# Block 1's first pair of a two-block transformer kernel: one low part by a negated cast and an accumulating DMA, two sums read from PSUM, another order in the lead-in

## The chip, the cores and the metric

One core of a Trainium2 chip runs the whole program in one launch. The metric is the device time of that core in microseconds (us). A profiled execution gives each engine's instructions with their times, counted from the first instruction of the span.

## The reference, cut to what matters

Two transformer blocks run one after the other on 256 tokens of width 1024, in float32. The change lies in block 1, whose two layers each have two SwiGLU feed-forwards around a mixer, so four feed-forwards in all:

```python
def _swiglu(x, w1, w3, w2):
    return (jax.nn.silu(x @ w1) * (x @ w3)) @ w2

for l in range(DEPTH):                                    # DEPTH = 2
    h = _swiglu(x, ffn_w1[l, 0], ffn_w3[l, 0], ffn_w2[l, 0])   # "which" 0
    x = _layernorm(ALPHA * x + 0.5 * h, ...)
    h = _mixer(x, l, ...)
    x = _layernorm(ALPHA * x + h, ...)
    h = _swiglu(x, ffn_w1[l, 1], ffn_w3[l, 1], ffn_w2[l, 1])   # "which" 1
    x = _layernorm(ALPHA * x + 0.5 * h, ...)
```

x is 256 x 1024, w1 and w3 are 1024 x 2816, w2 is 2816 x 1024.

## The kernel before, in words

**Every product is three.** A float32 operand is split in a high part (ScalarE casts it to fp32r) and a low part (VectorE subtracts the high part from the original and writes fp32r). TensorE then multiplies high by high, high by low and low by high. So every 1 MB unit of weights (128 partitions x 2048 values) costs one cast of ScalarE and one subtraction of VectorE before TensorE may use it. Weights go through a ring of four slots: `w_raw` (loaded by SyncE's queue), `w_high`, `w_low`. The semaphores `slot_full`, `slot_hi` and `slot_lo` count the three steps for each slot. SyncE's next load into a slot waits until the low part of the unit before is made.

**How a feed-forward is cut.** The 2816 hidden columns are 11 blocks of 256. Blocks 0, 1, 4, 7 and 10 are computed plainly: units `h0_0`, `h0_1` and so on hold w1 and w3 of a block and half of the rows (`_0` rows 0 to 511, `_1` rows 512 to 1023), and `d0` holds its rows of w2. The other six blocks are three groups of two, called quads. In a quad, the hidden products for both 128-token tiles and both halves of the rows are made by seven products and not eight, as in Strassen's and Winograd's method. Their weight units are b11, b21, v, x, w, y and b22. They come from four raw pieces that SyncE's queue loads beside the ring: R11 and R21 (of w1; tiles `buf_v` and `buf_q`), R12 and R22 (of w3; `buf_u` and `buf_val`). VectorE's `add_to` makes, in place in R11, the sums R11+R12 (for v), then +R22 (for x), then +R21 (for y). GpSimd makes R12+R22 (for w) with an accumulating DMA from `buf_val` into `buf_u` (line 712) once the first of these sums is done. So R11 as loaded must have been read for b11 before the first `add_to` may overwrite it.

**The forms.** The other operands of v, x, w and b22 are four combinations of the activations, the forms. VectorE's `whole` (line 2707) rebuilds x's transpose as high plus low in a quarter of `mix_param`, `combine` (2711) forms a difference or sum of two quarters, ScalarE casts it into `form_high` (1981) and VectorE makes `form_low` (2715).

**The lead-in.** This is the stretch of each feed-forward before and in its first quad: block 0 (hidden of token tile 0, then tile 1), block 1, the transposes of block 0's activations, d0, transposes of block 1, then b11, b21, v, x, d1 for tile 0, w, d1 for tile 1, y, b22. Each engine works through an order written out by hand:

- TensorE as just said. Block 1's tile 0 needs the low part of h1_0 and `multiply(0,0)`; its tile 1 needs `multiply(0,1)`; x and w need their own low parts, w also ScalarE's copy `term2` (line 2011).
- ScalarE: the casts of x's transpose for tile 1, Silu of block 0 tile 0 (`activate(0,0)`, line 1952), casts of h1_0 and h1_1 (1844), Silu of tile 1, casts of d0 and b11 (1942), four forms, then it waits for R21 and casts b21, then Silu of block 1 tile 0, the cast of the transposes (1957), Silu of tile 1, casts of v, x and the rest.
- VectorE: low parts of x's transpose (2510), two `whole`, `multiply(0,0)` (2682), low of h1_0 (2504), two `whole`, two `combine`, `multiply(0,1)`, low of h1_1, two `combine`, low of d0, form 0, `multiply(1,0)`, low of the transposes (2688), forms 1 to 3, low of b11 (2673), `multiply(1,1)`, `add_to` R12 (2678), low of b21, low of v, low of the transposes, `add_to` R22, low of x, low of d1, `add_to` R21, low of w, y and b22.
- GpSimd: for each feed-forward two loads of `ln_param`, then for each quad a wait for the first sum and for R22, and the DMA of line 712.

The transposes of x for token tile 1 lie in the PSUM banks `aux[:, 2, :]` and `aux[:, 3, :]` (rows 0 to 511 and 512 to 1023).

Of the kernel before, what the change touches and what calls it, by code (L numbers as in the profile page):

```python
# [10 lines left out]
ALU = mybir.AluOpType  # L11
ACT = mybir.ActivationFunctionType
# [74 lines left out]
FFN_UNIT, FFN_USES, FFN_LOADS, FFN_DONE = ffn_units()  # L87
# [154 lines left out]
def build(nc, a, out, stop=None):  # L242
    ctx = ExitStack()
    with ctx:
        def sb(name, shape, dt=F32):
            return ctx.enter_context(nc.sbuf_tensor(name, shape, dt))

        def sem(name):
            return ctx.enter_context(nc.semaphore(name))
# [4 lines left out]
        wlo = sb("w_low", [P, RING, UNIT], F32R)  # L254
# [16 lines left out]
        ident = sb("ident", [P, P])  # L271
# [12 lines left out]
        nz = sb("newton_t", [P, 48])  # L284
# [16 lines left out]
        def flat(t):  # L301
            return t[:, :, :].rearrange("p t d -> p (t d)")
# [7 lines left out]
        quarter = [flat(mix_par)[:, k * NC:(k + 1) * NC] for k in range(4)]  # L310
        term1, term2, term3, silu1 = quarter
        FORM_AT = (1, 0, 2, 3)
        R11, R21, R12, R22 = range(4)
        sum_raw = [flat(t) for t in (bv, bq, bu, bval)]
# [11 lines left out]
        aux = ctx.enter_context(nc.psum_tensor("aux", [P, 4, NC], F32))  # L326
# [4 lines left out]
        slot_lo = [sem(f"slot_lo{s}") for s in range(RING)]  # L331
# [3 lines left out]
        aux_read = [sem(f"aux_read{b}") for b in range(4)]  # L335
# [9 lines left out]
        r_full = [sem(f"r_full{r}") for r in range(4)]  # L345
        sum_done = sem("sum_done")
        w_sum = sem("w_sum")
        form_done = sem("form_done")
        form_hi = sem("form_hi")
        form_lo = sem("form_lo")  # L350
# [19 lines left out]
        ident_in = sem("ident_in")  # L370
# [101 lines left out]
        def ffn_n(l, which, s):  # L472
            return l * SLOT_LAYER[s] + (FFN_USES[s] + CH // 2) * which
# [8 lines left out]
        def ffn_unit(l, which, name):  # L482

            s, n = FFN_UNIT[name][0:2]
            return s, ffn_n(l, which, s) + n
# [5 lines left out]
        def quads_before(l, which, q):  # L491
            return QUADS * (2 * l + which) + q
# [170 lines left out]
        def _(pool):  # L663
# [41 lines left out]

            def sums_by_dma(l, which):

                for q in range(QUADS):
                    n = quads_before(l, which, q)
                    pool.wait_ge(sum_done, 3 * n + 1)  # L710
                    pool.wait_ge(r_full[R22], 16 * n + 16)
                    pool.dma_start(sum_raw[R12], sum_raw[R22], accum_op=ALU.add).then_inc(w_sum, 16)
# [41 lines left out]
            n = 0  # L754
# [1081 lines left out]
        def _(act):  # L1836
# [92 lines left out]
            def ffn1(l, which, tile1, next_tile0, mid):  # L1929

                aux0 = [c.k for c in n_aux]

                def used(name):
                    act.wait_ge(unit_used, ffn_done(l, which, name))

                def high_plain(name):
                    s, _, n, _ = FFN_UNIT[name]
                    high(s, ffn_load(l, which, s) + n)

                def high_sum(name, q, r):  # L1940
                    s = FFN_UNIT[f"{name}_{q}"][0]
                    nc.scalar.copy(whi[:, s, :], sum_raw[r]).then_inc(slot_hi[s], 1)  # L1942
# [7 lines left out]
                def activate(i, t):  # L1950
                    act.wait_ge(aux_full[t], aux0[t] + PLAIN.index(i) + 1)
                    nc.scalar.activation(act_b[:, t, 0:FB], aux[:, t, 0:FB], ACT.Silu).then_inc(act_done, 1)

                def plain_high_T(i):
                    act.wait_ge(aux_full[2], aux0[2] + FFN_T[i] + 1)
                    _, src, (k, tok) = place_pair(2, 0)
                    nc.scalar.copy(yTh[:, k, tok], src).then_inc(t_hi, 1)
# [7 lines left out]
                def last_high(t):  # L1965
                    act.wait_ge(aux_full[2 + t], aux0[2 + t] + FFN_AUX[2 + t])
                    nc.scalar.copy(yTh[:, 2:4, t * P:(t + 1) * P],
                                   aux[:, 2 + t, 0:2 * P].rearrange("p (f c) -> p f c", f=2)).then_inc(t_hi, 1)

                tile1()  # L1970
                aux0[2:] = [n_aux[2].k, n_aux[3].k]
                activate(0, 0)
                high_plain("h1_0")
                high_plain("h1_1")
                activate(0, 1)
                high_plain("d0")
                loaded(0, R11)
                high_sum("b11", 0, R11)
                for n in range(FORMS):
                    act.wait_ge(form_done, FORMS * (2 * l + which) + n + 1)  # L1980
                    nc.scalar.copy(form_h[:, n, :, :].rearrange("p k c -> p (k c)"), quarter[FORM_AT[n]])\
                        .then_inc(form_hi, 1)
                used("h1_0")
                loaded(0, R21)
                high_sum("b21", 0, R21)
                activate(1, 0)
                plain_high_T(0)
                activate(1, 1)
                summed(0, 1)
                high_sum("v", 0, R11)  # L1990
# [209 lines left out]
            l = L2  # L2200
# [295 lines left out]
        def _(dve):  # L2496
# [3 lines left out]
            V = nc.vector  # L2500
# [161 lines left out]
            def ffn1(l, which, tile1, k_norm, next_tile0, mid, half_first):  # L2662

                aux0 = []
                act0 = NT * len(PLAIN) * (2 * l + which)

                def low_plain(name):
                    low(*ffn_unit(l, which, name))

                def low_sum(name, q, r):  # L2670
                    s, n = ffn_unit(l, which, f"{name}_{q}")
                    dve.wait_ge(slot_hi[s], n + 1)
                    V.tensor_tensor(wlo[:, s, :], sum_raw[r], cast(whi[:, s, :]), ALU.subtract)\  # L2673
                        .then_inc(slot_lo[s], 1)

                def add_to(q, r, other):
                    dve.wait_ge(r_full[other], 16 * quads_before(l, which, q) + 16)
                    V.tensor_tensor(sum_raw[r], sum_raw[r], sum_raw[other], ALU.add).then_inc(sum_done, 1)  # L2678

                def multiply(i, t):  # L2680
                    dve.wait_ge(act_done, act0 + NT * PLAIN.index(i) + t + 1)
                    V.tensor_tensor(gate_b[:, t, 0:FB], act_b[:, t, 0:FB], aux[:, t, FB:2 * FB], ALU.mult)\
                        .then_inc(aux_read[t], 1)
# [20 lines left out]
                def whole(t, half, at):  # L2704

                    k, tok = slice(4 * half, 4 * half + 4), slice(t * P, (t + 1) * P)
                    V.tensor_tensor(quarter[at].rearrange("p (k c) -> p k c", k=4), cast(xTh[:, k, tok]),
                                    cast(xTl[:, k, tok]), ALU.add)

                def combine(at, one, two, op):  # L2710
                    V.tensor_tensor(quarter[at], quarter[one], quarter[two], op).then_inc(form_done, 1)  # L2711
# [7 lines left out]
                tile1()  # L2719
                dve.drain()  # L2720
                h0 = n_hi.k
                whole(1, 0, 0)
                whole(1, 1, 1)
                multiply(0, 0)
                low_plain("h1_0")
                whole(0, 0, 2)
                whole(0, 1, 3)
                dve.drain()
                combine(1, 0, 1, ALU.subtract)
                dve.drain()  # L2730
                combine(0, 2, 0, ALU.subtract)
                multiply(0, 1)
                low_plain("h1_1")
                combine(2, 1, 2, ALU.subtract)
# [6 lines left out]
                plain_low_T(0)  # L2741
                for n in range(1, FORMS):
                    form_low(n)
                low_sum("b11", 0, R11)
                multiply(1, 1)
                add_to(0, R11, R12)
                low_sum("b21", 0, R21)
                for q in range(QUADS):
# [326 lines left out]
            l = L2  # L3075
# [502 lines left out]
```

## Time and profile before

| what | value |
| --- | --- |
| median of 3 runs | 1946.69 us (1946.23 to 1947.9) |
| the profiled execution, its own time | 1946.73 us |
| its span, first to last instruction | 1944.7 us |
| TensorE busy | 1896.4 us, 98% of the span |
| VectorE busy | 1405.9 us, 72% |
| ScalarE busy | 1000.5 us, 51% |
| mean granted TensorE clock | 0.996 of full |
| lead-ins, about | 15 to 75, 455 to 512, 642 to 700, 1082 to 1140 us |

The time outside the span is 1946.73 - 1944.7 = 2.0 us. A line such as `466.87 1.90 ACT L1844 CAST w_high<-w_raw ...` in a timeline gives the start, the length, the engine (PE TensorE, DVE VectorE, ACT ScalarE, POOL GpSimd), the line of the kernel, and what is written and read; brackets give the idle time of the engine before it and what ended it. Neighbouring instructions of an engine overlap by about 0.1 us, so that a row "x2" of 3.70 us is two casts that start 1.80 us apart.

### The profile page before, as it was taken

Reading aid. Unit: us, or ns where it says so; the run is one execution under the profiler, and the core shown is the slowest. Engines: PE = TensorE matmul, PEld = TensorE weight load, DVE = VectorE, ACT = ScalarE, POOL = GpSimd, SP = SyncE. Lnnn points to the kernel's source line nnn. Section 1 sums busy time; section 2 is a strip of 40 time slices with the busy share of each in tenths; the row PEclk is TensorE's granted clock in tenths of the full one; section 3 lists DMA queues with packets and bytes.
Section 4 is the critical chain, followed back from the end, with each engine's and each line's share of the span. In section 5 each row is a group of like instructions: output and inputs, shape, how many; then the busy total and the mean of one; then the engine's idle time right before and its main releaser. Section 6 shows DMA issues by size and latency. Waiting matters only on the chain.

```text
span 1944.7 us, 23187 instructions
## 1 busy us (share of the span) xinstructions
PE 1896.4 (98%) x9016; PEld 1553.2 (80%) x9016; DVE 1405.9 (72%) x1599; ACT 1000.5 (51%) x1203; POOL 108.4 (6%) x176
## 2 busy tenths in 40 slices
PE   8999999999999999999999999989999999999999
PEld 6788788887788778878888778877788887778887
DVE  6887766778887888777667988878755466775545
ACT  4555444544555455543554455557544355654443
POOL 2001100000000000110000000011000000100000
PEclk9999999999999999999999999999999999999999
DMA  9764554447764666565345766365465555346542
GB/s 345 230 217 167 199 191 173 148 156 260 230 222 145 226 216 216 187 215 196 131 173 165 246 216 217 125 170 174 136 227 173 172 179 178 120 152 211 182 163 87
DMA packets 177729, 366.39 MB, mean 188 GB/s; under 512 B 7408, under 2 KB 51360, under 8 KB 176096
## 3 DMA queue, kind: packets, MB, share of 16 engines
q1 hardware_dynamic: 170512, 334.85, 49.9%
q0 software_dynamic: 7120, 30.21, 6.0%
q8 instruction: 66, 1.08, 0.2%
q14 instruction: 31, 0.25, 0.0%
HBM read 351.39 MB, written 1.05 MB: 181 GB/s over the span
## 4 chain that ended last, share of the span: by engine, by line
PE 82%; DVE 11%; ACT 3%; DVEq 2%; DMA 1%; issue 1%; SPq 0%; ACTq 0%
PE acc L834 49%; PE aux L834 16%; PE aux L1110 10%; DVE w_low L2504 3%; DVE w_low L2673 2%; DVE buf_v L2678 1%; PE aux L849 1%; DMA buf_q<-ffn_w 1%; ACT w_high L1942 1%; PE aux L945 1%; PE aux L1242 1%; DVEq L2556 1%; DVE xT_low L2510 1%; PE aux L1073 1%; DVE mix_param L2711 0%
## 5 line engine op out<-in xcount | busy, mean ns | idle before, releaser
L2504 DVE TENSOR_TENSOR w_low<-w_raw,w_high 128x2048 fp32r<-128x2048 f32 (+2 forms) x268 | 604.2, 2267 | 208.5 <-ACT w_high L1844 205.0
L1844 ACT CAST w_high<-w_raw 128x2048 fp32r<-128x2048 f32 (+2 forms) x268 | 502.9, 1893 | 249.4 <-PE acc L834 207.7
L834 PE MATMUL acc<-w_high,yT_high 128*128 128x512 f32 (+1 forms) x836 | 331.6, 397 | 3.0 <-DVE yT_low L2688 2.5
L834 PE MATMUL acc<-w_high,yT_low 128*128 128x512 f32 (+1 forms) x836 | 326.0, 390 | 0.0
L834 PE MATMUL acc<-w_low,yT_high 128*128 128x512 f32 (+1 forms) x836 | 325.6, 389 | 0.0
L834 PE MATMUL acc<-w_high,xT_high 128*128 128x512 f32 (+2 forms) x752 | 298.0, 396 | 7.0 <-DVE xT_low L2510 4.5
L834 PE MATMUL acc<-w_high,xT_low 128*128 128x512 f32 (+2 forms) x752 | 291.4, 388 | 0.0
L834 PE MATMUL acc<-w_low,xT_high 128*128 128x512 f32 (+2 forms) x752 | 291.1, 387 | 0.0
L834 PE MATMUL aux<-w_high,xT_high 128*128 128x512 f32 x576 | 229.9, 399 | 7.2 <-DVE w_low L2504 4.5
L834 PE MATMUL aux<-w_high,xT_low 128*128 128x512 f32 x576 | 225.3, 391 | 0.0
L834 PE MATMUL aux<-w_low,xT_high 128*128 128x512 f32 x576 | 224.7, 390 | 0.0
L834 PEld LDWEIGHTS acc<-w_high,yT_high 128*128 128x128 f32 x836 | 157.6, 188 | 38.5 <-issue 6.5
L834 PEld LDWEIGHTS acc<-w_high,yT_low 128*128 128x128 f32 x836 | 157.3, 188 | 32.9
L834 PEld LDWEIGHTS acc<-w_low,yT_high 128*128 128x128 f32 x836 | 157.8, 189 | 30.6
L834 PEld LDWEIGHTS acc<-w_high,xT_high 128*128 128x128 f32 x752 | 141.7, 188 | 41.0 <-DVE xT_low L2510 5.2
L1942 ACT CAST w_high<-buf_v 128x2048 fp32r<-128x2048 f32 x48 | 91.8, 1913 | 153.4 <-DVE buf_v L2678 110.4
L834 PEld LDWEIGHTS acc<-w_high,xT_low 128*128 128x128 f32 x752 | 141.6, 188 | 28.8
L834 PEld LDWEIGHTS acc<-w_low,xT_high 128*128 128x128 f32 x752 | 141.8, 189 | 26.2
L2673 DVE TENSOR_TENSOR w_low<-buf_v,w_high 128x2048 fp32r<-128x2048 f32 x48 | 109.9, 2289 | 55.6 <-ACT w_high L1942 55.6
L834 PEld LDWEIGHTS aux<-w_high,xT_high 128*128 128x128 f32 x576 | 108.5, 188 | 32.9 <-issue 8.5
L834 PEld LDWEIGHTS aux<-w_high,xT_low 128*128 128x128 f32 x576 | 108.4, 188 | 23.2
L834 PEld LDWEIGHTS aux<-w_low,xT_high 128*128 128x128 f32 x576 | 108.6, 189 | 20.9
(385 smaller groups left out, 2329.1 us busy)
## 6 DMA issues: line engine op xcount, KB each, us to landing
w_raw<-w_ff SPq DMA_DIRECT2D x64, 1024.0 KB
w_raw<-w_in SPq DMA_DIRECT2D x52, 1024.0 KB
w_raw<-ffn_w SPq DMA_DIRECT2D x44, 1024.0 KB
w_raw<-ffn_w SPq DMA_DIRECT2D x78, 512.0 KB
w_raw<-w_branch SPq DMA_DIRECT2D x16, 1024.0 KB
buf_v<-ffn_w SPq DMA_DIRECT2D x12, 1024.0 KB, 9.1
buf_u<-ffn_w SPq DMA_DIRECT2D x12, 1024.0 KB, 6.0
buf_q<-ffn_w SPq DMA_DIRECT2D x12, 1024.0 KB, 6.9
```

Of the source, the lines that this page charges most:

```text
L834: last = nc.tensor.matmul(dst, lhs[:, kt, tok], rhs(j), start=(kt == k_first and q == 0), stop=(kt == k_last and q == 2))
L849: last = nc.tensor.transpose(aux[:, b, k * P:(k + 1) * P], src[:, t, kt * P:(kt + 1) * P], ident[:])
L945: last = nc.tensor.transpose(aux[:, b, (2 * f + t) * P:(2 * f + t + 1) * P], gate_b[:, t, f0:f0 + P], ident[:])
L1073: last = nc.tensor.transpose(aux[:, b, (2 * f + t) * P:(2 * f + t + 1) * P], h[:, f0:f0 + P], ident[:])
L1110: last = nc.tensor.matmul(aux[:, b, :], lhs(k), rhs[:, s, k * NC:(k + 1) * NC], start=(first and k == 0 and n == 0), stop=(k == 3 and n == ...
L1242: last = nc.tensor.transpose(aux[0:width, b, (2 * k + t) * P:(2 * k + t + 1) * P], src(t, h), ident[:])
L1844: nc.scalar.copy(whi[:, s, 0:size], raw[:, s, 0:size]).then_inc(slot_hi[s], 1)
L1942: nc.scalar.copy(whi[:, s, :], sum_raw[r]).then_inc(slot_hi[s], 1)
L2504: V.tensor_tensor(wlo[:, s, 0:size], raw[:, s, 0:size], cast(whi[:, s, 0:size]), ALU.subtract)\
L2510: V.tensor_tensor(dst_l[:, k, tok], src, cast(dst_h[:, k, tok]), ALU.subtract)\
L2556: dve.drain()
L2673: V.tensor_tensor(wlo[:, s, :], sum_raw[r], cast(whi[:, s, :]), ALU.subtract)\
```

## The change

- GpSimd and ScalarE make the low part of `b11_0`, the b11 of a feed-forward's first quad: ScalarE writes -R11, cast to fp32r, into the `w_low` slot, then a DMA that GpSimd issues adds R11 onto it. GpSimd waits until that DMA has landed and then raises `slot_lo`. VectorE's `low_sum("b11", 0, R11)` is gone, and VectorE waits for that `slot_lo` before `add_to(0, R11, R12)`.
- Of the four `whole` of VectorE the two for tile 1 are gone. ScalarE copies `aux[:, 3, :]` into a quarter, and two subtractions of VectorE read `aux[:, 2, :]` directly.
- ScalarE runs a Silu on one column of `ident` ahead of the lead-in, and casts h1_0 before `activate(0,0)`. VectorE takes h1_0's low part before `multiply(0,0)`.
- ScalarE does `activate(1,0)` and the cast of the transposes before it waits for R21 and casts b21. Its wait for `h1_0` used is gone.
- VectorE does `multiply(1,1)` right after the forms.

```diff
@@ GpSimd, sums_by_dma
+                n = 2 * l + which
+                s = FFN_UNIT["b11_0"][0]
+                pool.wait_ge(b11_neg, n + 1)
+                pool.dma_start(wlo[:, s, :], sum_raw[R11], accum_op=ALU.add).then_inc(b11_sum, 16)
+                pool.wait_ge(b11_sum, 16 * n + 16)
+                pool.sem_inc(slot_lo[s], 1)
@@ ScalarE, ffn1
+                act.wait_ge(ident_in, 16)
+                nc.scalar.activation(nz[:, 0:1], ident[:, 0:1], ACT.Silu)
                 tile1()
                 aux0[2:] = [n_aux[2].k, n_aux[3].k]
+                high_plain("h1_0")
                 activate(0, 0)
-                high_plain("h1_0")
+                act.wait_ge(aux_read[3], aux0[3] + 1)
+                nc.scalar.copy(quarter[1], aux[:, 3, :]).then_inc(form_in, 1)
                 high_plain("h1_1")
                 activate(0, 1)
                 high_plain("d0")
                 loaded(0, R11)
                 high_sum("b11", 0, R11)
+                nc.scalar.activation(wlo[:, FFN_UNIT["b11_0"][0], :], sum_raw[R11], ACT.Copy, scale=-1.0)\
+                    .then_inc(b11_neg, 1)
                 for n in range(FORMS):
...
-                used("h1_0")
+                activate(1, 0)
+                plain_high_T(0)
                 loaded(0, R21)
                 high_sum("b21", 0, R21)
-                activate(1, 0)
-                plain_high_T(0)
                 activate(1, 1)
@@ VectorE, ffn1
-                whole(1, 0, 0)
-                whole(1, 1, 1)
+                low_plain("h1_0")
                 multiply(0, 0)
-                low_plain("h1_0")
                 whole(0, 0, 2)
                 whole(0, 1, 3)
+                dve.wait_ge(form_in, 2 * l + which + 1)
+                V.tensor_tensor(quarter[1], aux[:, 2, :], quarter[1], ALU.subtract).then_inc(form_done, 1)
                 dve.drain()
-                combine(1, 0, 1, ALU.subtract)
-                dve.drain()
-                combine(0, 2, 0, ALU.subtract)
+                V.tensor_tensor(quarter[0], quarter[2], aux[:, 2, :], ALU.subtract).then_inc(form_done, 1)
                 multiply(0, 1)
...
                     form_low(n)
-                low_sum("b11", 0, R11)
                 multiply(1, 1)
+                s, n = ffn_unit(l, which, "b11_0")
+                dve.wait_ge(slot_lo[s], n + 2)
                 add_to(0, R11, R12)
                 low_sum("b21", 0, R21)
```

## Rows read from the trace of the kernel before

**Rows 1.** Whole page, busy time and share of the span of TensorE.

```profile
PE 1896.4 (98%) x9016; PEld 1553.2 (80%) x9016; DVE 1405.9 (72%) x1599; ACT 1000.5 (51%) x1203; POOL 108.4 (6%) x176
```

**Rows 2.** Waits of TensorE: total, times, longest (us), whole span.

```profile
PE aux L1110 <- DVE w_low L2673: 10.0, 4, 2.8
...
PE aux L834 <- DVE w_low L2504: 4.5, 5, 1.1
...
PE acc L834 <- DVE yT_low L2688: 2.5, 1, 2.5
...
PE aux L1110 <- ACT mix_param L2011: 2.2, 2, 1.1
```

**Rows 3.** Timeline of VectorE, second lead-in: start, length, engine, line.

```profile
461.44 0.69 DVE L2510 TENSOR_TENSOR xT_low<-aux,xT_high 128x512 fp32r<-128x512 f32 x1 [1.06 <-ACT xT_high L1849]
...
464.93 2.29 DVE L2504 TENSOR_TENSOR w_low<-w_raw,w_high 128x2048 fp32r<-128x2048 f32 x1 [1.08 <-ACT w_high L1844]
467.14 1.29 DVE L2707 TENSOR_TENSOR mix_param<-xT_high,xT_low 128x512 f32<-128x512 f32 x2
...
479.61 2.28 DVE L2673 TENSOR_TENSOR w_low<-buf_v,w_high 128x2048 fp32r<-128x2048 f32 x1
...
482.14 2.29 DVE L2678 TENSOR_TENSOR buf_v<-buf_v,buf_u 128x2048 f32<-128x2048 f32 x1
...
493.61 2.29 DVE L2673 TENSOR_TENSOR w_low<-buf_v,w_high 128x2048 fp32r<-128x2048 f32 x1 [1.98 <-ACT w_high L1942]
```

**Rows 4.** Timeline of ScalarE, second lead-in.

```profile
461.42 1.28 ACT L1952 ACT_TABLE_LOAD   x1
...
463.00 3.70 ACT L1844 CAST w_high<-w_raw 128x2048 fp32r<-128x2048 f32 x2
466.60 0.38 ACT L1952 ACTIVATE buf_k<-aux 128x256 f32<-128x256 f32 x1
466.87 1.90 ACT L1844 CAST w_high<-w_raw 128x2048 fp32r<-128x2048 f32 x1
```

**Rows 5.** Timeline of TensorE, second lead-in.

```profile
467.37 0.47 PE L834 MATMUL aux<-w_high,xT_high 128*128 128x512 f32 x1 [1.11 <-DVE w_low L2504]
```

**Rows 6.** Stages: PE, PEld, DVE, ACT, POOL busy, clock, DMA share, GB/s.

```profile
474.00:477.00 3.00, 3.00 (x17) 2.51 (x16) 2.95 (x3) 3.00 (x4) 0.00 (x0) 1.00 0.84 341
486.00:491.00 5.00, 5.00 (x24) 4.13 (x23) 5.00 (x4) 0.85 (x2) 0.00 (x0) 1.00 1.03 210
498.00:500.00 2.00, 2.00 (x7) 1.51 (x6) 2.00 (x2) 0.00 (x0) 0.00 (x0) 0.50 0.26 29
```

**Rows 7.** Line L712, the accumulating DMA, all twelve.

```profile
DMA to landing us min/median/max: 6.9/7.0/8.7
```

**Rows 8.** Timeline of GpSimd, second lead-in.

```profile
484.73 0.90 POOL L712 DMA_DIRECT2D buf_u<-buf_val  x1 [24.34 <-DVE buf_v L2678]
```

**Rows 9.** DMA issues of 459 to 461 us.

```profile
ln_param<-ln_g POOLq DMA_DIRECT2D x1, 512.0 KB, 6.8
ln_param<-ln_b POOLq DMA_DIRECT2D x1, 512.0 KB, 8.7
```

**Rows 10.** DMA issues, whole span.

```profile
ln_param<-mix_norm POOLq DMA_DIRECT2D x1, 512.0 KB, 4.1
```

**Rows 11.** Timeline of ScalarE, first lead-in.

```profile
28.24 1.92 ACT L1942 CAST w_high<-buf_v 128x2048 fp32r<-128x2048 f32 x1
...
35.35 1.90 ACT L1942 CAST w_high<-buf_q 128x2048 fp32r<-128x2048 f32 x1 [3.12 <-DMA buf_q<-ffn_w]
```

**Rows 12.** Timeline of VectorE, first lead-in.

```profile
42.98 2.29 DVE L2678 TENSOR_TENSOR buf_v<-buf_v,buf_u 128x2048 f32<-128x2048 f32 x1
```

**Rows 13.** Timeline of ScalarE, third lead-in.

```profile
655.77 1.91 ACT L1844 CAST w_high<-w_raw 128x2048 fp32r<-128x2048 f32 x1
```

**Rows 14.** Timeline of VectorE, third lead-in.

```profile
669.76 2.29 DVE L2678 TENSOR_TENSOR buf_v<-buf_v,buf_u 128x2048 f32<-128x2048 f32 x1
```

**Rows 15.** Timeline of VectorE, fourth lead-in.

```profile
1108.76 2.28 DVE L2678 TENSOR_TENSOR buf_v<-buf_v,buf_u 128x2048 f32<-128x2048 f32 x1
```

More of the change, by code:

```diff
@@ L347, in build @@
         w_sum = sem("w_sum")
+        b11_neg = sem("b11_neg")
+        form_in = sem("form_in")
+        b11_sum = sem("b11_sum")
         form_done = sem("form_done")
```

## The prediction

> **What bounds the kernel now.** I read the page first: TensorE is busy for 98% of the span [rows 1], so only its waits, under 50 us, can be had. The list of TensorE's waits then says where they are [rows 2]. Four of them, 10.0 us in all, one in each feed-forward, are before product x of the first quad (line 1110, waiting for the low part of line 2673). Twice the copy of line 2011 holds w for 1.1 us. Block 1 waits for the low part of h1_0 for 1.1 us in three lead-ins (the second one's is [rows 5]), and once d0 waits for 2.5 us (first lead-in). Together this is about 18 us, the most that the change can touch: 0.9%.
>
> The timelines of VectorE and ScalarE of the second lead-in [rows 3, 4] say what is behind the wait before x. VectorE adds R12 to R11 from 482.14; from there to the end of x's low part at 493.61 + 2.29 = 495.90 it is a fixed chain of 13.8 us: add, low of b21, low of v, low of the transposes, add, ScalarE's cast of x, low of x. The product w hangs on the same chain one `add_to` and one cast later. The change alters nothing in this chain. So **a lead-in becomes shorter by what its first `add_to` (line 2678) comes earlier**, and by nothing else, as long as TensorE still waits for x. Call its start A: it is 42.98, 482.14, 669.76 and 1108.76 in the four lead-ins [rows 3, 12, 14, 15]. The second and fourth are one pattern, 626.6 us apart.
>
> **The parts that make TensorE's early waits go.** ScalarE's table load of 1.28 us, now between the cast of x's transpose and the Silu [rows 4], moves into idle time ahead of the lead-in; if it couldn't be hidden there it would cost what it costs now. With h1_0's cast ahead of the Silu too, that cast starts at about 461.4 and not 463.00, and the low part ends at 465.6, before TensorE ends block 0 at 467.37 - 1.11 = 466.26 [rows 5]. The wait of 1.1 us goes, in three lead-ins. The third has no such wait and gains nothing here. VectorE's two `whole` (0.60 us each by the pair of [rows 3]) become one ScalarE copy that fits between two casts; reading PSUM in a subtraction costs VectorE no more than SBUF: its low part of x's transpose reads PSUM and takes 0.69 us [rows 3], and I take the same for the new subtractions (bounds 0.6 and 0.7, no matter for the sum). All this puts TensorE up to 1.4 us ahead in block 1. But what goes here comes back before x, unless A moves as well.
>
> The Trainium skill (ScalarE: Activation LUTs, What ACT_TABLE_LOAD costs) gives a switch of tables 2.66 us, load and drain. Here the Silu begins right behind the 1.28 us, so the trace has no such drain; by the page's figure the early wait would shrink by 1.4 us more, and the sum would be the same.
>
> **The part that moves A.** VectorE loses the low part of b11, 2.20 us of its time (line 2673 at 479.61, [rows 3]). In its place A waits for this chain, second lead-in: TensorE ends block 0 at 466.3; Silu of tile 1 to 466.6, as before [rows 4]; then casts at a spacing of 1.80 us (the pair of 3.70 us in [rows 4]): d0 from 466.6, b11 from 468.4, the negated cast from 470.2 to 472.1. The trace has no negated cast; a plain one of this size takes 1.90, and I take that. (Bounds: 1.9, and 2.3 if it were as slow as VectorE's.) Then 0.3 us until GpSimd begins the DMA, as now from the end of the add at 484.43 to 484.73 [rows 3, 8]; T for the DMA to land; and 0.3 us, my estimate from the same step, for GpSimd to raise the semaphore. So A = 472.7 + T. Without this DMA VectorE would be free by 480: its forms end at 479.61 already before, and everything ahead of them is earlier. So T decides as soon as it is over 7.3 us.
>
> **T.** The same kind of DMA, same size, same engine, landed 6.9 to 8.7 us after its issue, median 7.0 [rows 7]. Those run in stretches where nothing is loaded: in 486 to 491 us the DMA engines are full (1.03) with it alone, at 210 GB/s [rows 6]. It is 5 us of all the engines' time, twice what a load of 1 MB costs (341 GB/s at a share of 0.84 in 474 to 477). The new one starts at 472.4 in the second lead-in, where the loads of d2 and d3 want most of the engines. Below, T is 7.0. Above, with even sharing against loads all the time, it is 7.0 + 5 = 12. Between them: if turns go by bytes, the loads get a third, 2.5 us more, so 9.5; if the turns favour the transfer with the larger pieces, less. Two `ln_param` loads on the same queue, put into a full DMA at 459, landed after 6.8 and 8.7 us [rows 9], one in a quieter place after 4.1 [rows 10]: they don't stand in line behind SyncE's loads, they push in. I take T = 8.4, both ends kept for the range.
>
> **The sum.** Second lead-in: A = 481.1 for 482.14, **1.0 us won**. Fourth, the same pattern: **1.0 won**. Third: ScalarE's cast of d0 is at 655.77 [rows 13] and doesn't come earlier, as TensorE doesn't there; the negated cast ends at 655.77 + 3.60 + 1.91 = 661.3, A = 661.9 + 8.4 = 670.3 for 669.76, **0.5 lost**. First: b11's cast starts at 28.24 [rows 11], held by d0's arrival, which doesn't change, so the negated cast ends at 31.95 and T = 8.4 would give A = 41.0, 2.0 earlier. But R21 is on its way then: it landed at 35.3, ScalarE waited 3.12 us for it [rows 11]. With 5 us of DMA work pushed in ahead of it it lands at 40.3; the cast of b21 is over at 42.2, `activate(1,1)` is queued behind it on ScalarE, `multiply(1,1)` behind that, and VectorE gets to A at 42.9 to 43.0, for 42.98: **nothing won**. (If R21 isn't held up: 2.0 more.) There the new order does make d0 start about 3 us earlier, for `activate(1,0)` no longer stands behind R21, and TensorE stands before the transposes and x instead.
>
> Total: 1.0 + 1.0 - 0.5 + 0 = 1.5 us. In general the second to fourth lead-ins give 26.8 - 3T: 5.8 us at T = 7.0, nothing at 8.9. TensorE's own wait for b11's low part is met in time: from 466.3 it has 72 products at about 0.22 us (24 in 5 us, [rows 6]) and eight short transposes to do first, so it gets there at about 483.4. Queued behind VectorE's new wait are the low parts of b21 and v, which TensorE needs 4.4 and 6.6 us after A: 485.6 and 487.8, before it gets there at 486.2 and 488.9, twelve products apart. The next DMA of GpSimd (line 712) needs the first sum anyway, so it isn't held up. R22 and the loads behind it have many us to spare in the last three lead-ins.
>
> TensorE's clock: after the wait before x it fell to 0.50, the lower of its two levels (1.2 and not 2.4 GHz), in 498 to 500 us [rows 6]. In the new kernel the wait before x is about 0.4 us longer in the second and fourth, so the low clock can come in more lead-ins. As w then waits less for its copy (1.1 us where the clock stayed, [rows 2]), this costs some tenths of a us each; I leave it out of the sum and in the range.
>
> From the profiled execution's 1946.73 (span 1944.7 and 2.0 around it; the median of the runs is 1946.69, the same within 0.04): 1946.73 - 1.5 = **1945.2 us**.
>
> **Rivals.** (1) *The DMA is as quick as its median, T = 7.0.* For it speaks that the loads leave gaps at 0.84; against it, that none of the twelve rows behind that median shares the engines with loads. It gives 5.8 us, 1940.9; with R21 not held up A is 39.6 in the first lead-in, 3.4 more, 1937.5. Down to T = 7.6 or with R21 on time the kernel is faster by over 0.2% (3.9 us). Chance 0.3. (2) *The DMA shares evenly and becomes the bound,* T = 11: A is 483.7, 672.9 and 1110.3, and 43.6 in the first, so 1.6 + 3.1 + 1.6 + 0.6 = 6.9 us lost, 1953.6. It is one mechanism: VectorE, which has the low parts of b21 and v queued behind, stands for a transfer. It is slower than before from T = 8.9 and by over 0.2% from 10.2. Chance 0.15, as no row shows this DMA beside loads. The Trainium skill (DMA: Bandwidth & Descriptors, Queues, rings and completion order) says that each DMA engine goes round between the queues it has work for, a packet at a time. By that rule, even turns in time would give this rival's 1953.6; that the software queue isn't held behind SyncE's agrees with [rows 9]. (3) *It does nothing:* the gains of the early part are given back before x and A moves by less than a us each way; this is my forecast's case, with chance 0.55.
>
> **Numbers.** 0.2% of 1946.7 is 3.9 us, about what a measurement of this kernel can tell from no change. Faster 0.3, within 0.55, slower 0.15. The likeliest case's own range is 1942.8 to 1948. The range to hold 8 in 10 takes in most of rival 1 and the start of rival 2: 1938.5 to 1950.8.
>
> **What would show it.** Right: no wait of TensorE for h1_0's low part; VectorE idle for 2 to 3 us before line 2678 in the last three lead-ins, released by GpSimd; the new DMA landing in 8 to 9 us; x waiting 2.5 to 3.5 us. In the first lead-in ScalarE waits for R21 until about 40. Wrong: a landing near 7 or over 10, R21 on time, or a wait before x that vanishes, which would mean that the chain from A isn't fixed.

## The result: slower, outside the predicted range

The changed kernel takes 1952.03 us (median of 13 runs, 1949.54 to 1955.25), the kernel before 1947.50 beside it (13 runs, 1946.23 to 1948.48): a ratio of 1.0024, 95% interval 1.0016 to 1.0033. That is 4.5 us slower. I had forecast 1945.2 in 1938.5 to 1950.8, and gave "slower" a chance of 0.15. The profiled execution took 1950.31 us, 3.6 more than that of before; over the 13 runs TensorE's mean granted clock goes from 0.990 to 0.996, and the profiled one (0.996) is among the quickest.

The page after, TensorE against [rows 1]; TensorE's work is the same, its waits are not:

```profile
span 1948.5 us, 23191 instructions
...
PE 1896.9 (97%) x9016; PEld 1553.3 (80%) x9016; DVE 1392.4 (71%) x1587; ACT 1010.2 (52%) x1215; POOL 113.6 (6%) x180
```

TensorE's waits after, to be laid beside [rows 2] (in total, times, longest; lines 843 and 1119 were 834 and 1110 before):

```profile
PE aux L1119 <- DVE w_low L2687: 18.4, 8, 3.6
...
PE acc L843 <- DVE w_low L2518: 3.4, 4, 2.0
...
PE aux L1119 <- POOLq L716: 2.0, 2, 1.6
PE aux L843 <- DVE w_low L2518: 1.2, 2, 0.6
```

The early part of the change did what it should: the wait for h1_0's low part (now line 2518) fell from 4.5 to 1.2 us in the group of [rows 2], and the copy that held w (2.2 us) is gone from the list. All of it came back, and more, at the products of the first quad: 10.0 us became 18.4. Of these, 14.2 us are the four waits before x (3.5 to 3.6 us each, for 2.0 to 2.8 before) and 4.2 us are four new ones before b21. On top, b11 waits for the new DMA itself in the first and the third lead-in (1.6 and 0.4 us, the row with POOLq). The waits of VectorE name the new holder, four times, once in each feed-forward:

```profile
DVE buf_v L2692 <- POOLq L716: 17.9, 4, 5.3
```

Line 2692 is the `add_to` whose start I called A (2678 before), and line 716 is where GpSimd raises `slot_lo`, once the new DMA has landed. The DMA's own line:

```profile
L714 POOL DMA_DIRECT2D w_low<-buf_v x4: 878/898/917, 32.1 to 1101.8; - x4
...
DMA to landing us min/median/max: 9.6/10.6/11.5
```

That is T: 9.6 to 11.5 us, median 10.6, for the 8.4 of my sum. The timeline of VectorE gives A itself, for [rows 12, 3, 14, 15] (in brackets the idle time before, and what ended it):

```profile
43.28 2.29 DVE L2692 TENSOR_TENSOR buf_v<-buf_v,buf_u 128x2048 f32<-128x2048 f32 x1 [5.30 <-POOLq L716]
...
482.13 2.29 DVE L2692 TENSOR_TENSOR buf_v<-buf_v,buf_u 128x2048 f32<-128x2048 f32 x1 [3.41 <-POOLq L716]
...
672.77 2.29 DVE L2692 TENSOR_TENSOR buf_v<-buf_v,buf_u 128x2048 f32<-128x2048 f32 x1 [5.28 <-POOLq L716]
...
1112.00 2.29 DVE L2692 TENSOR_TENSOR buf_v<-buf_v,buf_u 128x2048 f32<-128x2048 f32 x1 [3.94 <-POOLq L716]
```

The lead-ins themselves begin 0.06, 1.25 and 2.79 us later than before from the second on, by the start of TensorE's transposes. In each lead-in's own time A has moved by +0.30, -0.07, +1.76 and +0.45 us: 2.4 of the 3.8 us by which the span grew. The rest is at product x and behind it: x's twelve products take 1.57, 0.90 and 1.59 us longer in the first, second and fourth lead-in (0.07 less in the third), against which w's two waits of 1.1 us are gone. Here is x in TensorE's timeline of the second lead-in and in the stages with its clock (columns as in [rows 6]):

```profile
496.04 0.76 PE L1119 MATMUL aux<-w_high,form_high 128*128 128x512 f32 x1 [3.54 <-DVE w_low L2687]
```

```profile
496.00:498.00 2.00, 1.96 (x5) 1.60 (x6) 2.00 (x1) 1.65 (x1) 0.00 (x0) 0.50 0.04 8
498.00:500.00 2.00, 2.00 (x6) 1.53 (x5) 2.00 (x2) 0.00 (x0) 0.00 (x0) 0.50 0.24 48
500.00:502.00 2.00, 2.00 (x6) 1.59 (x5) 2.00 (x2) 1.59 (x1) 0.00 (x0) 0.51 1.02 343
```

After an idle 3.54 us the clock is at its lower level (0.50) for all of x in this lead-in. x's twelve products took 5.46 us (496.04 to 501.50), for 4.56 before, where the same wait was 2.66 us and the first four products still ran at full clock. This lead-in lost 1.19 us although A had not moved at all.

What the steps ahead of T did, in the timeline of ScalarE (compare [rows 4]):

```profile
453.32 1.28 ACT L1980 ACT_TABLE_LOAD   x1 [2.25 <-PE acc L843]
...
461.36 1.92 ACT L1853 CAST w_high<-w_raw 128x2048 fp32r<-128x2048 f32 x1
...
468.43 1.91 ACT L1951 CAST w_high<-buf_v 128x2048 fp32r<-128x2048 f32 x1
470.24 1.91 ACT L1992 ACTIVATE w_low<-buf_v 128x2048 fp32r<-128x2048 f32 x1
```

The table load is hidden, h1_0's cast starts at 461.36 (forecast 461.4), the negated cast takes 1.91 us and ends at 472.15 (forecast 472.1). GpSimd issues at 472.45, 0.3 us later, as assumed. Up to there every step is in its place; the transfer is not.

### The profile page after: what moved, and what is told of

It is laid out like the page before. It is cut to its first block, busy times and chain, and to the rows that moved or that the text cites. A ratio compares the mean times of both kernels' runs of the same rounds, so it can differ in the third digit from the quotient of the medians.

```text
span 1948.5 us, 23191 instructions
## 1 busy us (share of the span) xinstructions
PE 1896.9 (97%) x9016; PEld 1553.3 (80%) x9016; DVE 1392.4 (71%) x1587; ACT 1010.2 (52%) x1215; POOL 113.6 (6%) x180
## 4 chain that ended last, share of the span: by engine, by line
PE 80%; DVE 8%; issue 5%; DMA 3%; ACT 3%; DVEq 1%; POOL 0%; SPq 0%; POOLq 0%
PE acc L843 48%; PE aux L843 16%; PE aux L1119 9%; DMA w_low<-buf_v 2%; DVE w_low L2518 2%; DVE w_low L2687 1%; DVE buf_v L2692 1%; PE aux L858 1%; DMA w_raw<-ffn_w 1%; ACT w_high L1951 1%; PE aux L954 1%; PE aux L1251 1%; DVEq L2570 1%; DVE xT_low L2524 1%; PE aux L1082 0%
## 5 line engine op out<-in xcount | busy, mean ns | idle before, releaser
L2687 DVE TENSOR_TENSOR w_low<-buf_v,w_high 128x2048 fp32r<-128x2048 f32 x44 | 100.8, 2290 | 55.9 <-ACT w_high L1951 55.9
```

## The experiments

Each kernel ran beside the kernel before on one chip; "A" is given for the first to the fourth lead-in. In one table:

```
kernel             median us  ratio, 95% interval       landing, us       A, us
after              1952.03    1.0024 [1.0016, 1.0033]   11.1 9.6 11.5 10.1   43.28 482.13 672.77 1112.00
e1 no DMA          1938.11    0.9954 [0.9940, 0.9967]   -                    37.91 475.21 662.69 1100.01
e2 DMA alone       1957.23    1.0052 [1.0038, 1.0066]   11.1 to 12.0         42.77 484.75 675.43 1116.62
e3 loads held      1939.16    0.9962 [0.9948, 0.9975]   10.4 7.0 7.0 7.0     42.49 478.73 663.44 1099.55
e4 order alone     1939.19    0.9963 [0.9949, 0.9977]   -                    38.14 476.20 662.57 1100.40
e6 R21 order alone 1943.91    0.9983 [0.9974, 0.9992]   -                    39.34 478.72 665.03 1103.92
e7 h1_0 alone      1944.10    0.9986 [0.9977, 0.9995]   -                    43.89 481.78 668.25 1105.78
e8 half the DMA    1940.77    0.9968 [0.9955, 0.9981]   8.4 to 9.4           40.31 477.62 665.64 1102.31
e9 loads held late 1941.07    0.9973 [0.9962, 0.9983]   11.2 7.0 8.9 6.9     43.58 479.71 666.32 1102.50
e5 mixed           1934.32    0.9933 [0.9920, 0.9947]   - 7.0 7.0 6.9        37.75 473.96 660.19 1096.32
```

The kernel before had 1946.91 beside e1 to e4, 1947.26 beside e5 to e8 and 1946.72 beside e9. Landings and A are those of the one profiled execution of each kernel. The theory is that the DMA, late beside the loads, sets A and takes more than the rest gains; the rival, that the new order in the lead-in is what costs.

**e1: everything but the DMA.** VectorE makes the low part again, ahead of `multiply(1, 1)`.

```diff
-                nc.scalar.activation(wlo[:, FFN_UNIT["b11_0"][0], :], sum_raw[R11], ACT.Copy, scale=-1.0)...
...
+                low_sum("b11", 0, R11)
                 multiply(1, 1)
...
-                dve.wait_ge(slot_lo[s], n + 2)
```

> The changed kernel without the negated cast and the accumulating DMA: VectorE makes b11's low part itself again, all other edits stay. Theory (the DMA alone costs, through the start A of the first add_to): VectorE is free when its forms are done, adds 2.2 us for the low part, and A comes 3.4 us earlier than in the kernel before in the first lead-in and 1.2 to 1.4 us in each of the other three, so about 7 us less than before: 1940 us, if TensorE's low clock does not appear more often. Rival (the new orders or the reads of PSUM cost): the time stays at 1950 to 1952 us.

It gave 1938.11, 8.8 us faster than the kernel before beside it. As the whole change is 4.5 us slower, its DMA costs 13.3 us. A comes 5.1, 6.9, 7.1 and 8.8 us earlier than before; most of it is won in the first lead-in and carried on. In each lead-in's own time it is 4.7, 1.6, 1.5 and 1.6 us, more than the 3.4 and 1.2 to 1.4 expected. Waits of TensorE:

```profile
PE aux L1113 <- DVE w_low L2679: 11.1, 4, 3.2
```

So x still waits, 2.65 us in the last three. The wait was moved there and not removed, but from an A that is earlier.

**e2: the DMA alone**, put into the kernel before: the negated cast after `high_sum("b11", 0, R11)`, GpSimd's five lines, and VectorE's wait in the place of `low_sum("b11", 0, R11)`.

> The kernel before with nothing but the negated cast and the accumulating DMA in place of VectorE's low part of b11. Theory (the DMA alone costs): it is issued within 0.3 us of where the changed kernel issues it in the second and third lead-in, lands 9.6 to 11.5 us later, and the time is that of the changed kernel, 1950 to 1952 us. Rival (the new orders cost): VectorE is relieved of 2.2 us and the time is 1946 to 1948 us, no more than before.

It gave 1957.23, 10.3 us slower than before and 5 more than the theory's upper figure. The direction is settled, the size was a miss: here all four landings are over 11 us (11.1, 12.0, 11.5, 11.8), not only the first and third. In the second and fourth lead-in SyncE issues a load of 1 MB 0.16 us ahead of the DMA here, 1.38 us ahead of it in the changed kernel; the table under e9 shows what that does.

```profile
DMA to landing us min/median/max: 11.1/11.6/12.0
```

**e3: the DMA with the loads behind it held back.** SyncE waits for the sum before the loads that stand behind R22.

```diff
                     quad_load(l, which, 0, r)
+                sp.wait_ge(b11_sum, 16 * (2 * l + which) + 16)
                 for q in range(QUADS):
```

> The changed kernel, where the sync engine waits for the new DMA before it issues the first load behind R22, so that in the last three lead-ins no weight load is under way beside it. Theory (loads beside it stretch it): it lands 7.0 us after issue in the last three lead-ins, A comes 2.5 to 4.5 us earlier there than in the changed kernel, and with about the same first lead-in the time is 1942 to 1944 us. Rival (this DMA is slow by itself, for its fp32r destination or its place): it still takes 9.6 us or more and the time stays at 1950 us or above.

It gave 1939.16, better than expected. The DMA's line and VectorE's A (second lead-in):

```profile
DMA to landing us min/median/max: 7.0/7.0/10.4
```

```profile
478.73 2.29 DVE L2693 TENSOR_TENSOR buf_v<-buf_v,buf_u 128x2048 f32<-128x2048 f32 x1 [0.74 <-POOLq L717]
```

One wait on the queue of loads, and the same DMA lands in 7.0 us in the last three lead-ins. In the first it can't help: what is under way there stands ahead of the wait, and the landing is 10.4 us. VectorE's idle time ahead of A is 0.74 us, where it was 3.4 to 5.3. And x waits 1.4 to 1.5 us in these three, with its products at full clock (0.47 us for the first one, for 0.76 above):

```profile
492.64 0.47 PE L1120 MATMUL aux<-w_high,form_high 128*128 128x512 f32 x1 [1.46 <-DVE w_low L2688]
```

In each lead-in's own time A comes 0.7, 2.7, 4.5 and 3.2 us earlier than in the changed kernel, 11.0 of the 12.3 us by which the span is shorter; the rest would be x's products.

The wait on the queue is not free. The held loads are now issued just ahead of GpSimd's next DMA, the one that makes w's sum (now line 722), and in the second lead-in that lands after 12.7 us, for the 7.0 of [rows 7]:

```profile
DMA to landing us min/median/max: 12.7/12.7/12.7
```

ScalarE waited 1.7 us for it, and no wait of TensorE names it. And e3 is not faster than e1, which has no such DMA (1938.11): what the quiet DMA gains over VectorE's low part in the last three lead-ins it loses in the first.

**e4: the order alone.** e1 with the four `whole` copies and the SBUF subtractions of the kernel before in the place of the sums from PSUM.

> As e1, and the two sums are made from the rebuilt transposes again as before (four wholes, no copy by ScalarE, no read of PSUM): only the orders and the early table load are left of the change. Theory: the two wholes for tile 1 lie in the time in which VectorE waits for the cast of h1_0, so this kernel is within 1 us of e1. Rival: the sums from PSUM save VectorE 1.2 us in each lead-in, so this kernel is 4 to 5 us slower than e1.

It gave 1939.19, so reading PSUM directly is worth 1.1 us, and the new order 7.7. The 1.1 is small: the intervals of the two ratios overlap, though all five runs of e1 (up to 1938.53) lie below all five of e4 (from 1938.83).

**e6 and e7: the order in two halves**, each put into the kernel before. e6 has `activate(1, 0)` and `plain_high_T(0)` ahead of the wait for R21; e7 has the table load and h1_0's cast ahead of the Silu, and `low_plain("h1_0")` ahead of `multiply(0, 0)`.

```diff
-                used("h1_0")
-                loaded(0, R21)
-                high_sum("b21", 0, R21)
                 activate(1, 0)
                 plain_high_T(0)
+                loaded(0, R21)
+                high_sum("b21", 0, R21)
```

> The kernel before with one edit: ScalarE does the Silu and the cast of the transposes of block 1's tile 0 before it waits for R21. Theory: only the first lead-in gains, as only there R21 is late; VectorE's idle 3.8 us before that tile's product goes and A comes 3.5 to 5 us earlier: 1942 to 1943.5 us. Rival (the gain of e4 is from the early cast of h1_0): no change, 1946 to 1947 us.

> The kernel before with only the early table load and h1_0's cast and low part ahead of the first Silu and product. Theory: nothing in the first lead-in (R21 sets A there) and up to 1.3 us earlier A in the second and fourth, about 0 in the third: 1944 to 1945.5 us. Rival (the waits that go come back before x): no change, 1946 to 1947 us.

They gave 1943.91 (0.4 over the expected range) and 1944.10, 3.3 and 3.2 us won; e4, which has both, has 7.7, 1.2 more than the two added up. e6's gain is in the first lead-in, whose A is at 39.34 for 42.98, and stays at 3.4 to 4.8 in the later ones. In e7 the first A is even 0.9 later, but in this profile the first weights came late and TensorE's first transposes of the lead-in began 1.7 us later too, so in the lead-in's own time A is 0.8 earlier; the others gain 1.2, 1.0 and 1.2 (about 0 was expected in the third). I had written that what goes in block 1 comes back before x unless A moves, and then counted as if A stayed. It doesn't: VectorE's last work ahead of A is `multiply(1, 1)`, which waits for block 1's products, so A moved with them.

**e8: half the bytes.** The DMA makes 512 KB of the low part, VectorE the other half.

```diff
-                pool.dma_start(wlo[:, s, :], sum_raw[R11], accum_op=ALU.add).then_inc(b11_sum, 16)
+                pool.dma_start(wlo[:, s, 0:D], sum_raw[R11][:, 0:D], accum_op=ALU.add).then_inc(b11_sum, 16)
...
+                pool.wait_ge(b11_half, n + 1)
```

> The changed kernel where ScalarE negates and the DMA adds only half of b11's low part (512 KB) and VectorE makes the other half (1.1 us). If the late start of the DMA's data is a fixed price beside loads (3 to 4 us from issue to first data, as in the changed kernel's trace, and then by size), it lands after 6.5 to 7.5 us; if all of it stretches with the size, after 5 to 5.5 us. In both cases A comes 3 to 5 us earlier than in the changed kernel in each lead-in, and the time is 1938 to 1941 us.

The time came out as expected (1940.77), the landing not: 8.4 to 9.4 us for half the bytes, where the whole takes 7.0 with no loads beside it. Nor did A: in each lead-in's own time it comes 3.2, 1.5, 1.3 and 2.5 us earlier than in the changed kernel, where 3 to 5 was expected. So its own bytes are not the main part of what makes the landing long: halving them takes off 0.7 to 2.4 us. The trace's packet records show where the time is. From GpSimd's issue to the DMA's first data packet, from there to its last one, and what SyncE's loads moved in between:

```
kernel, issue at       first packet   data     loads meanwhile
after        32.10     +4.28          6.33     0.57 MB
after       472.45     +2.86          6.28     0.50
after       661.24     +4.35          6.48     0.63
after      1101.80     +2.74          6.89     0.69
e3          471.70     +1.47          5.19     0
e3          656.39     +1.45          5.17     0
e8 (half)   468.60     +4.40          4.02     0.63
e8 (half)   656.12     +4.41          4.58     0.83
```

With the engines to itself the DMA's first packet comes 1.5 us after its issue and its data take 5.2 us. Beside the loads it starts 1.3 to 2.9 us later, and the whole DMA then runs 1.1 to 1.7 us longer. The stages around it say the same (second lead-in, the last two columns are DMA share and GB/s):

```profile
473.00:474.00 1.00, 1.00 (x6) 0.83 (x5) 1.00 (x1) 1.00 (x3) 0.36 (x1) 1.00 0.97 395
474.00:475.00 1.00, 1.00 (x8) 0.85 (x7) 1.00 (x2) 0.54 (x2) 0.00 (x0) 1.00 1.04 422
...
476.00:477.00 1.00, 1.00 (x7) 0.79 (x5) 1.00 (x3) 1.00 (x1) 0.00 (x0) 1.00 1.11 233
477.00:478.00 1.00, 1.00 (x6) 0.84 (x5) 1.00 (x3) 0.63 (x2) 0.00 (x0) 1.00 1.02 213
...
481.00:482.00 1.00, 1.00 (x7) 0.81 (x6) 0.00 (x0) 0.00 (x0) 0.00 (x0) 1.00 0.96 393
```

At 395 to 422 GB/s the loads run alone, though the DMA was issued at 472.45; at 213 to 233, with the engines just as full, it is the new DMA's turn. Compare e3, where 474 to 476 is this DMA alone:

```profile
474.00:476.00 2.00, 2.00 (x12) 1.68 (x10) 1.85 (x4) 1.95 (x3) 0.00 (x0) 1.00 0.97 197
```

**e9: the wait of e3, two loads later**, so that the loads of d2 and d3 may still be under way.

```diff
                     hidden1(l, which, o, 0)
+                    if q == 0:
+                        sp.wait_ge(b11_sum, 16 * (2 * l + which) + 16)
                     for name in late_downs(q):
```

> As e3, but the sync engine's wait stands two loads later: d1 and h4_0 (2 MB) may go out beside the new DMA, only d2 and d3 are held back. In the second and fourth lead-in h4_0 is through at about the issue of the new DMA, in the third it runs 2 to 3 us longer. If only loads that run beside it stretch the new DMA, it lands after 7.0 to 7.5 us in the second and fourth and after 8.5 to 9.5 us in the third, and the time is 1939.5 to 1942 us, with e3's 1939.2 below. If d2 and d3 were not what held it up (rival: any backlog of the loads' queue does, or the DMA's own price), it lands after 9 us or more in all, and the time is 1947 us or more.

All of it came as expected: 7.0 and 6.9 us in the second and fourth lead-in, 8.9 in the third, 1941.07 us. By the packet records nothing of the loads was left beside the transfer in the second and fourth, and 0.10 MB in the third. The place in the program is the same as in the changed kernel; the loads under way are what differs.

The same records show what the start hangs on. In the second and fourth lead-in the last load that SyncE issued ahead of the DMA stands at another distance in each kernel, and the first packet follows it:

```
kernel   last load issued ahead of the DMA by   first packet of the DMA after its issue
e9       6.43 us                                1.47  1.46 us
after    1.38                                   2.86  2.74
e8       0.52                                   4.40  4.37
e2       0.16                                   5.04  5.09
```

In the changed kernel's second lead-in the 256 packets of 4 KB of that load (1 MB, issued at 471.07) run from 472.1 to 476.0, and the DMA's first one comes at 475.3. The load issued 2.2 us *after* the DMA stands back in turn: no load has a packet under way from 476.2 to 478.9. In the third lead-in more of the loads is still to be moved, and the first packet comes at 4.3 to 4.4 us in the changed kernel, e2 and e8.

**e5: what the runs point to.** The first feed-forward makes the low part on VectorE (as e1), the other three by the DMA with the loads held back (as e3).

```diff
+                if (l, which) == (0, 0):
+                    low_sum("b11", 0, R11)
                 multiply(1, 1)
+                if (l, which) != (0, 0):
+                    s, n = ffn_unit(l, which, "b11_0")
+                    dve.wait_ge(slot_lo[s], n + 2)
```

> The first feed-forward as in e1 (VectorE makes b11's low part, no negated cast, no DMA), the other three as in e3 (DMA, with the loads behind R22 waiting for it). Theory (each lead-in's share follows its A alone): A comes at 37.9 in the first lead-in as in e1, 4.6 us earlier than in e3, the rest stays as in e3: 1934 to 1935.5 us, below every kernel so far. Rival (the first lead-in's gain is given back later, or e1 and e3 gain the same microseconds): 1938 us or more.

It gave 1934.32, ratio 0.9933 [0.9920, 0.9947]: 12.9 us faster than before where the change as it was made is 4.5 slower, and the best kernel of this study. Its page, TensorE's waits and VectorE's A (second lead-in):

```profile
PE 1892.9 (98%) x9016; PEld 1552.2 (80%) x9016; DVE 1394.1 (72%) x1588; ACT 1009.1 (52%) x1214; POOL 112.7 (6%) x179
```

```profile
PE aux L1122 <- DVE w_low L2691: 7.6, 4, 3.0
...
PE aux L1122 <- ACT mix_param L2029: 3.3, 3, 1.1
```

```profile
473.96 2.29 DVE L2696 TENSOR_TENSOR buf_v<-buf_v,buf_u 128x2048 f32<-128x2048 f32 x1 [0.80 <-POOLq L719]
```

TensorE's wait before x is 7.6 us in all, for 14.2 in the changed kernel, 11.1 in e1 and 10.0 before. w waits 1.1 us for its copy three times, where it was twice before and not at all in the changed kernel.

## Why the prediction was wrong

**The step that failed is T, the landing time of the new DMA, 8.4 in the sum.** It was 9.6 to 11.5. I had taken it between its quiet 7.0 and an even sharing of the engines with the loads, which adds 5 us, and went below the middle, since two smaller loads in [rows 9] "push in". Both ends priced only how the engines are shared, once both transfers move. That this part has the right size is luck: the data took 1.1 to 1.7 us longer, and 8.4 had 1.4 for it. What I had no term for is that the first packet comes 1.3 to 2.9 us later while loads are under way. The rows had a hint of it: 512 KB took 6.8 us in a full DMA [rows 9] and 4.1 in a quieter place [rows 10], 2.7 us more for half the bytes. I read them for the order in which transfers run and not for the delay. With the four measured landings in the place of 8.4 the recorded sum loses 0.7, 0.2, 3.6 and 0.6 us and gives 1951.8, against 1950.31 in the profiled run: T alone turns the forecast from faster to slower.

**Which rival it was.** The second: the DMA becomes what VectorE waits for, with T near 11. A follows at once: issue plus landing is 472.45 + 9.6 = 482.05 for A at 482.13, and the other three agree to 0.1 us (the 0.3 us that I added for GpSimd's semaphore isn't there). The rival's 1953.6 was for T = 11 in all four; the landings were 11.1, 9.6, 11.5 and 10.1, and the profiled run has 1950.31. Its mechanism, even sharing of the engines' time, was not what happened: in the time of the DMA's 128 packets of 8 KB ran 136 to 184 of the loads', mostly 4 KB at 0.16 to 0.17 us each. Where both transfers move, they go about one for one: from 478.8 to 480.3 us start 31 packets of the DMA and 31 of the loads. With one such turn for each of the DMA's packets, 16 engines would need 128 / 16 x 0.17 = 1.4 us more, an estimate that falls in the 1.1 to 1.7 measured. It isn't shown to be the cause of all of it: the data took 6.50 us in e9's third lead-in with 0.10 MB of loads beside them, and two of the twelve transfers behind [rows 7] took 6.65 and 6.81 us with none, each with its last one to three packets well after the rest.

The Trainium skill (DMA: Bandwidth & Descriptors, Queues, rings and completion order) describes turns between the queues, a packet at a time, and those one-for-one stretches agree with it; I had priced them as equal time, 5 us. The start does not come out of turns: in the 1.3 to 2.9 us by which it is late the DMA gets none, while the loads' packets run.

**The first lead-in.** I wrote that R21 would be pushed back to 40.3 and set A at 43.0. R21 landed at 35.3, as before; ScalarE waited 0.73 us for it:

```profile
35.34 1.91 ACT L1951 CAST w_high<-buf_q 128x2048 fp32r<-128x2048 f32 x1 [0.73 <-DMA buf_q<-ffn_w]
```

The new DMA's first packet came at 36.4, once R21 was in. R21 went first, and the DMA waited for its turn. A came out at 43.28 for my 43.0, a right number by luck, for a wrong reason: T was 11.1 and set it alone.

**The third lead-in.** I had written that ScalarE's cast of d0 (655.77) "doesn't come earlier". It began at 655.42, though the lead-in itself began 1.25 us later (0.85 by its second group of transposes), so in its own time it was 1.2 to 1.6 us early. The DMA was issued at 661.24 and not 661.6, and T = 11.5 took that back and more. e7, which has the early cast of h1_0 alone, also brings A 1.0 us forward in this lead-in, where I had nothing.

**Behind A.** I had b11, b21 and v in time for TensorE. With T = 11.1 and 11.5 b11 is late itself (1.6 and 0.4 us), and b21 is late in all four lead-ins, by 0.3 to 1.5 us.

**VectorE's idle time.** In the first lead-in VectorE stood free from 37.98, the end of its last work ahead of A, and idle for 5.3 us; in e1, with the low part of b11 to make as well, it begins A at 37.91.

**The clock.** I left it out as some tenths of a us in each lead-in. The second one lost 1.19 us with A unmoved, 0.9 of it in x's products, and x's products of the first and fourth, at full clock before, lost 1.6 us each, most of which the missing wait of w gave back. Over the span 1.4 of the 3.8 us are not in A. The runs' mean clock, 0.990 to 0.996, goes with their times (1955.25 us at 0.990, 1949.98 at 0.996), and the median lies 1.7 us above the profiled run. That more lead-ins have low stretches in the other runs would explain it, but only the profiled one has a trace.

**The early part** I had put at nothing, on the ground that only A counts. That A counts is right in the main, but VectorE's work ahead of A follows block 1's products, so an earlier block 1 moves A: e7 gains 3.2 us by it. And R21's order alone, which brings A from 42.98 to 39.34 in the first lead-in (e6), gains 3.3. So there were 8.8 us to win and 13.3 to lose where the sum had 1.5 to win in all. It could not show that, as it had no line for where A would be without the DMA. "VectorE would be free by 480" stood in the text (it was free at 478.72) and was never priced as the alternative.

**What held:** the fixed chain from A to x's low part, 13.8 us (482.13 to 493.60 + 2.29 = 495.89); the ends of the casts in the second lead-in, to 0.1 us; the hidden table load; the 0.3 us step ahead of the DMA; and that x's wait would take back what block 1's lost. The PSUM sums (1.1 us by e1 and e4) are small, as I had them.

Why the first packet is late: the rows fit loads issued earlier being worked off first. It comes 1.5 us after issue with none left, 2.1 with a little left (third lead-in of e9) and, in the second and fourth lead-in, 2.7 to 2.9, 4.4 and 5.0 to 5.1 as the last load is issued 1.38, 0.52 and 0.16 us ahead of it. e8's 4.4 us for half the bytes says that the delay isn't in the size of the DMA. Open is what in the chip puts them in this order, and how the delay grows with several loads ahead: these distances came about by the other edits, and no run varied them alone.

## What to carry to other kernels

A transfer that a busy engine waits on is to be priced at its landing beside the loads that are queued at that moment, its start as well as its bytes; the quiet median of the same line is only its lower end. If nothing urgent is behind those loads, one wait on the loading queue gives the quiet time back (9.6 to 11.5 us became 7.0 here) and turns a loss of 4.5 us into a gain of 7.8 (e3). Look then at what the held loads meet next (a DMA of 12.7 us here), and compare with leaving the transfer out (8.8, e1): it paid once it was used only in the lead-ins that give the quiet time (12.9, e5). And each part of a change is to be priced against the chain as it is without the other parts.

## What was unexpected of the hardware

- A GpSimd-issued accumulating DMA of 1 MB has its first data packet 1.5 us after issue with no loads beside it, 2.7 to 4.3 us with them (4.2 to 5.1 in e2), and 4.4 us when it has half the bytes. A load of another queue, issued 0.16 us ahead, goes first with nearly all of its 1 MB.
- Once it moves, it takes most of the engines: its data need 6.3 to 6.9 us for 5.2 alone, and the loads get through 0.5 to 0.7 MB in that time, where they ran at about 400 GB/s just before.
- After waits of 1.4 to 1.6 us before x all of its products ran at full clock (eight lead-ins of e3, e5 and e9, 0.47 us for the first); after waits of 2.6 to 3.6 us some ran at 0.50 at once (0.76 us for the first), some began at full clock (0.47) and fell, and some kept it for all twelve (e9's first, after 3.58 us).
